# Two float32-split matmul layers on one core: the modulation's shift of the raw attention projections added on ScalarE, and the last slab's two output tiles made one behind the other

## The reference

```
def modulate(h, shift, scale):
    return h * (1 + scale[:, None, :]) + shift[:, None, :]
...
    mod = c_act @ w_mod[l] + b_mod[l]
    sh1, sc1, ga1, sh2, sc2, ga2, sh3, sc3, ga3 = jnp.split(mod, N_MOD, axis=-1)
    h = modulate(rms_norm(x, g_ffn1[l]), sh1, sc1)
    x = x + 0.5 * (1 + ga1[:, None, :]) * swiglu(h, w1_gate[l], w1_up[l], w1_down[l])
    h = modulate(rms_norm(x, g_mix[l]), sh2, sc2)
    x = x + (1 + ga2[:, None, :]) * hybrid_mixer(h, w_in[l], b_f[l], g_q[l], g_k[l], w_o[l])
    h = modulate(rms_norm(x, g_ffn2[l]), sh3, sc3)
    x = x + 0.5 * (1 + ga3[:, None, :]) * swiglu(h, w2_gate[l], w2_up[l], w2_down[l])
```

## Time and profile before

| what | value |
|---|---|
| median of 3 runs | 819.49 us (819.26 to 819.83) |
| profiled execution, its own time | 819.52 us |
| its span | 817.3 us |
| busy: TensorE matmul, VectorE, ScalarE | 802.3, 644.4, 487.0 us |
| qkv3 and o3, 495 to 620: TensorE, VectorE, ScalarE busy | 121.5, 93.4, 79.0 of 125 us |
| TensorE's granted clock | 1.00 in every stretch |

### The profile page before, as it was taken

The page is one execution under the profiler, slowest core; times in us unless marked ns, Lnnn a source line. Parts: engine busy times, 40 slices in busy tenths (PEclk is TensorE's granted clock), DMA queues, the critical chain, the costliest instruction groups (busy, mean ns, idle before and its releaser), DMA issues.

```text
span 817.3 us, 16917 instructions
## 1 busy us (share of the span) xinstructions
PE 802.3 (98%) x6862; PEld 780.7 (96%) x6862; DVE 644.4 (79%) x1333; ACT 487.0 (60%) x1015; POOL 21.2 (3%) x53
## 2 busy tenths in 40 slices
PE   7999999999999999999999999899999999999998
PEld 7999998999999999999999999889889999999998
DVE  5788887888899887999988786977667896775551
ACT  6754566767767565756554556665655775555440
POOL 1000000000000000000000000700000000000000
PEclk9999999999999999999999999999999999999999
DMA  8777673765565998489998887545334578665540
GB/s 290 260 234 226 200 267 128 235 199 188 189 225 166 324 308 286 144 295 336 361 333 292 288 263 222 167 134 175 120 118 156 156 249 274 207 199 194 194 155 27
DMA packets 150013, 179.44 MB, mean 220 GB/s; under 512 B 5680, under 2 KB 139568, under 8 KB 149936
## 3 DMA queue, kind: packets, MB, share of 16 engines
q1 hardware_dynamic: 147680, 177.22, 65.8%
q10 hardware_dynamic: 1232, 1.11, 0.4%
q0 software_dynamic: 1024, 0.03, 0.1%
HBM read 177.27 MB, written 1.05 MB: 218 GB/s over the span
## 4 chain that ended last, share of the span: by engine, by line
PE 77%; DVE 4%; ACT 2%; issue 1%; DVEq 0%; ACTq 0%
PE bank L1349 24%; PE bank L1352 24%; PE bank L1353 24%; DVE wlo L970 1%; PE bank L1451 1%; PE bank L1439 1%; PE bank L1468 0%; PE bank L1370 0%; PE bank L1402 0%; DVE yb L1010 0%; PE bank L1418 0%; DVE A L1021 0%; ACT B L748 0%; PE bank L1395 0%; ACT sq L768 0%
## 5 line engine op out<-in xcount | busy, mean ns | idle before, releaser
L970 DVE TENSOR_TENSOR wlo<-raw,whi 128x512 fp32r<-128x512 f32 x528 | 342.7, 683 | 69.4 <-ACT whi L727 68.7
L727 ACT ACTIVATE whi<-raw 128x512 fp32r<-128x512 f32 x528 | 307.3, 622 | 97.1 <-PE bank L1353 85.2
L1349 PE MATMUL bank<-A,whi 128*128 128x256 f32 x1264 | 357.3, 283 | 3.4 <-DVE wlo L970 2.6
L1352 PE MATMUL bank<-A,whi 128*128 128x256 f32 x1264 | 350.6, 277 | 0.1
L1353 PE MATMUL bank<-A,wlo 128*128 128x256 f32 x1264 | 350.2, 277 | 0.0
L1349 PEld LDWEIGHTS bank<-A,whi 128*128 128x128 f32 x1264 | 237.7, 188 | 6.5 <-DVE wlo L970 3.5
L1352 PEld LDWEIGHTS bank<-A,whi 128*128 128x128 f32 x1264 | 237.7, 188 | 1.2 <-issue 1.0
L1353 PEld LDWEIGHTS bank<-A,wlo 128*128 128x128 f32 x1264 | 237.8, 188 | 0.0
L1349 PE MATMUL bank<-Hhi,whi 128*128 128x256 f32 x528 | 146.2, 277 | 0.0
L1353 PE MATMUL bank<-Hhi,wlo 128*128 128x256 f32 x528 | 145.9, 276 | 0.0
L1352 PE MATMUL bank<-Hlo,whi 128*128 128x256 f32 x528 | 145.9, 276 | 0.0
(11 more groups left out here) (150 smaller groups left out, 811.0 us busy)
## 6 DMA issues: line engine op xcount, KB each, us to landing
mring<-in_w_mod SPq DMA_DIRECT2D x72, 512.0 KB, 6.4
raw<-in_ffn_w_up SPq DMA_DIRECT2D x22, 1024.0 KB, 5.1
raw<-in_w_gate SPq DMA_DIRECT2D x22, 1024.0 KB, 5.7
raw<-in_w_up SPq DMA_DIRECT2D x22, 1024.0 KB, 6.0
raw<-in_w_down SPq DMA_DIRECT2D x16, 1024.0 KB, 5.4
raw<-in_w_in SPq DMA_DIRECT2D x12, 1024.0 KB, 5.4
raw<-in_moba_w_qkv SPq DMA_DIRECT2D x11, 1024.0 KB, 5.5
raw<-in_ffn_w_down SPq DMA_DIRECT2D x8, 1024.0 KB, 6.2
```

The costliest lines, as they stand in the source:

```text
L727: act.activation(whi[:, i % SPL, k0:k1, 0:width], raw[:, i % RAW, k0:k1, 0:width], ACT.Copy).then_inc(s_whi, 1)
L970: dve.tensor_tensor(lo, raw[:, i % RAW, k0:k1, 0:width], hi.bitcast(F32), ALU.subtract).then_inc(s_wlo, 1)
L1349: pe.matmul(o, hi, xh, start=kg == 0 and not (j and halved(g)), stop=False)
L1352: pe.matmul(o, hi, xl, start=False, stop=False)
```

## The change

In a raw group of qkv, VectorE now multiplies by Rr and the scale in one instruction, and copies the two columns of the shift, scaled, from PSUM to a small tile shiftc. The bank is free behind that. ScalarE adds the column as a bias, in place on the QKV tiles, in a step of its own, `shift`, which the plan puts two turns behind the group's end, behind that turn's weight steps and ahead of `attend`: shift 69 behind hi 89 3, shift 70 behind hi 90 3, shift 71 behind hi 91 3 and so ahead of scores 16. TensorE's scores and V transpositions of raw groups now wait for these additions too.

In the last slab TensorE makes output tile 6 over all six k-tiles and then tile 7. VectorE adds tile 6 to x when it is ready, and tile 7 at the end.

```
 def evict(g):                                   # plan
             if tag == "qkv":
                 st.put("evict", g, 0)
+                if g in self.unnormed:
+                    shifts.append((g, turns[0]))
...
                     if i > 0:
                         fill(pieces(tag, c0, kt))
+                    while shifts and shifts[0][1] < turns[0]:
+                        st.put("shift", shifts.pop(0)[0])
                     attend()
...
+        shiftc = sb("shiftc", [P, 4, 2])
...
+        raw_g = {g: k for k, g in enumerate(g for g, x in enumerate(groups) if g in unnormed and x[1] == "qkv")}
...
+        def in_place(need, g):
+            emptied(need, g)
+            if g in raw_g:
+                need.wait_ge(s_biased, 2 * raw_g[g] + 2)
...
+            def add_shift(g):                   # ScalarE
+                base = qkv_base(groups[g][0], groups[g][2])
+                emptied(need, g)
+                for i in range(2):
+                    x = QKV[:, place(groups[g][0], base) + i, :]
+                    act.activation(x, x, ACT.Identity, bias=shiftc[:, raw_g[g], i:i + 1]).then_inc(s_biased, 1)
...
             def evict(g, part):                 # VectorE
-                if part == 0 and g not in by_silu:
+                if g == len(groups) - 1:
+                    need.wait_ge(s_ahead, 1)
+                elif part == 0 and g not in by_silu:
                     need.wait_ge(s_chunk, chunk_of_group(g))
...
                     for i in range(2):
-                        dve.tensor_tensor(QKV[:, place(ph, base) + i, :], at(g, i), Rr[:, 0, :], ALU.mult).then_inc(s_scaled, 1)
+                        dve.scalar_tensor_tensor(out=QKV[:, place(ph, base) + i, :], in0=at(g, i), scalar=scl,
+                                                 in1=Rr[:, 0, :], op0=ALU.mult, op1=ALU.mult).then_inc(s_scaled, 1)
                     for i in range(2):
-                        o = QKV[:, place(ph, base) + i, :]
-                        need.wait_ge(s_scaled, 2 * mul_g[g] - 1 + i)
-                        ins = dve.tensor_scalar(o, o, at(g, i, S, S + 1), scl, ALU.add, ALU.mult)
+                        ins = dve.tensor_scalar(shiftc[:, raw_g[g], i:i + 1], at(g, i, S, S + 1), scl, None, ALU.mult)
                     ins.then_inc(s_evicted, 1)
...
                         else:                   # down4's eviction
+                            if n == KD - 1:
+                                need.wait_ge(s_chunk, chunk_of_group(g))
...
+            def last_slab(i, kt):               # TensorE
+                ph, tag, c0, k0, nk = slabs[i][:5]
+                g = plan.group_of[i]
+                for j, k in [(0, kt)] + [(1, k) for k in range(nk if kt == nk - 1 else 0)]:
+                    final = k == nk - 1
+                    xh, xl, ncol = here(tag, ph, k0 + k, g)
+                    hi = whi[:, i % SPL, k, j * P:j * P + P]
+                    lo = wlo[:, i % SPL, k, j * P:j * P + P]
+                    o = at(g, j, 0, ncol)
+                    pe.matmul(o, hi, xh, start=False, stop=False)
+                    pe.matmul(o, hi, xl, start=False, stop=False)
+                    ins = pe.matmul(o, lo, xh, start=False, stop=final)
+                    if j == 0 and final:
+                        ins.then_inc(s_ahead, 1)
+                    elif final or (j == 0 and k % 2 == 1):
+                        ins.then_inc(s_chunk, 1)
...
             def scores(n):
-                emptied(need, max(qkv_group[ph, f], qkv_group[ph, 8 + f]))
+                for tile in sorted((f, 8 + f), key=lambda t: qkv_group[ph, t]):
+                    in_place(need, qkv_group[ph, tile])
...
             def v_turn(ph, tile):
-                emptied(need, qkv_group[ph, tile])
+                in_place(need, qkv_group[ph, tile])
```

More of the change, by code:

```diff
@@ L195, in lay @@
         offer(2)
-        pending, waiting, flight, scaling = [], [], [], []
+        pending, waiting, flight, scaling, shifts = [], [], [], [], []
         turns = [0]
@@ L503, in build_program @@
         s_xeven, s_xscaled = sem("s_xeven"), sem("s_xscaled")
+        s_ahead, s_biased = sem("s_ahead"), sem("s_biased")
         s_cond, s_cact, s_msum, s_mod = sem("s_cond"), sem("s_cact"), sem("s_msum"), sem("s_mod")
@@ L834, in evict @@
                     if ph == "qkv3" and (4 <= base < 8 or 12 <= base < 16):
-                        emptied(need, g)
+                        in_place(need, g)
                         if nth("qkn", base) > 1:
@@ L953, in _ @@
                        "ccol": condition, "evict": evict, "fpart": forget, "scores": first_passes, "turn": turned, "later": later,
-                       "values": values, "vturn": v_turned, "qkn": qk_norm}
+                       "values": values, "vturn": v_turned, "qkn": qk_norm, "shift": add_shift}
             for step in st.list:
@@ L1343, in multiply @@
                     pe.matmul(banks[NORM_BANK][:, 511:512], meanf[:, :], meanf[:, 0:1], start=True, stop=True)
+                if i == len(slabs) - 1:
+                    last_slab(i, kt)
+                    return
                 for j in range(1 if tag == "f" else 2):
```

## The result

| | before | after |
|---|---|---|
| median | 819.38 us (4 runs, 819.06 to 819.83) | 829.07 us (4 runs, 829.04 to 830.64) |
| profiled execution, own time | 819.52 us | 830.64 us |
| its span | 817.3 us | 828.3 us |

The ratio is 1.0119, with a 95% interval of 1.0106 to 1.0131: the changed kernel is 1.2% slower, 9.7 us, where I had forecast 819.9 us.

What follows compares the result with a forecast made beforehand. TensorE, busy 98% of the 817.3 us span, was taken as the bound. 819.49 + 0.83 (qkv3) - 0.39 (last slab) = 819.9 us, not distinguishable from no change; range 818.2 to 820.9.

Steps and rivals of the forecast that it cites:

- Behind it: qkv3 after the transposition: ScalarE 0.92 us later, product loses 0.60 us, norm product 0.83 in all; shiftc's move counted as none.
- The two signs of being wrong: qkv3: the forecast would be wrong if the transposition came before 525.6 or the product near 531 did not wait.
- VectorE's and ScalarE's prices: qkv3's raw groups: 0.80 us of VectorE per group, 0.40 less than today; 0.82 us of ScalarE per pair of additions.
- The sum up to the transposition: qkv3: TensorE's first wait shrinks, but waits for the shifts return the gain; transposition at 526.05, exactly where it is today.
- the forecast instants: qkv3 start times: scores 523.07, transposition 526.05, product 531.24, norm product 544.95.
- The last slab: Kernel's end: last addition and store 0.4 us earlier, -0.4 us; landing unchanged, up to 0.2 more possible; order most likely free.
- (1): Rival, qkv3: ScalarE not in the way, VectorE's lead reaches TensorE, both waits shrink; 817.1 us; chance 0.13.
- (2): Rival, qkv3: columns cost VectorE as much as today's additions, 0.27 us each; slower, 821.1 us; 0.09 for loss over 1.6 us.
- (3): Rival, qkv3: a pause absorbs the shift's delay, so qkv3 gives 0 and the tail 0.4; 819.1 us; chance 0.25.
- (4): Rival, qkv3: first wait's 0.8 us survive to the end, second wait keeps its length; 818.3 us; chance 0.10.

Runs made afterwards that it cites:

- e2: Kernel before with only an unused 32-byte tile where shiftc lies; 829.11 us against 820.49, ratio 1.0110.
- e1: Changed kernel with the pad ahead of H 32 bytes shorter, so H and O return to their old places; 820.57 us against 820.49, ratio 1.0004.
- g1: Changed kernel with tiles back in place and group 71's shift done by VectorE in the eviction, as before; 820.00 us against 820.13, ratio 0.9998.
- e3: Kernel before with only the last slab's new order, no shiftc; 818.73 us against 820.49, ratio 0.9984.
- g2: g1 with group 71's shift, and TensorE's wait for it, left out altogether; 819.81 us against 820.13, ratio 0.9995.
- f3: Kernel before with A alone moved 32 bytes on, to -32 from the weights, H and O unmoved; 843.52 us against 820.17, ratio 1.0285.
- f2: Kernel before with weights whi and wlo moved 64 bytes on, so A, H and O lie at -128; 844.82 us against 820.17, ratio 1.0301.
- f1: Kernel before with every tile moved by 64 bytes, weights and moving tiles alike; 820.18 us against 820.17, ratio 0.9994.
- f6: Kernel before with H and O moved back by 32 bytes, to -96; 827.50 us against 819.43, ratio 1.0087.
- f5: Kernel before with H and O moved on by 128 bytes, to +64; 826.83 us against 819.43, ratio 1.0089.
- f4: Kernel before with H and O moved back by 64 bytes, to -128; 829.13 us against 820.17, ratio 1.0110.
- e4: Kernel before with H and O moved on by 64 bytes, to 0 from the weights; 831.70 us against 820.49, ratio 1.0140.

## Why the prediction was wrong

**The step that failed** is the last sentence of "Behind it": "The new tile shiftc takes 32 bytes and moves the tiles declared behind it; no row shows an effect of a tile's place, and I count none." I saw the move and priced it at nothing, with no bound. H lies at a single distance in the trace of before, so no row there could give its price. But that is a reason to leave the sum open by the tile's share of the matmuls: H carries 1584 of the 6862, so each 1% on its interval is worth 1.8 us. It was 4.4%, 7.9 us, which is more than all other terms together. The runs put in its place: a move of H and O by 32 bytes relative to the weights costs 8.6 us by itself (e2), and moving them back takes it away (e1). A row of before could have warned me. Matmuls over B, whose k-tiles lie at eight places, are longer than those over A (120.3 ns from start to start for 113.4 in up2), by more than their two further columns on 256 (0.8%) would suggest. No run says whether the places or the columns do it. The means of the page are 284 and 277 ns:

```profile
L1352 PE MATMUL bank<-A,whi 128*128 128x256 f32 x1264 | 350.6, 277 | 0.1
...
L1352 PE MATMUL bank<-B,whi 128*128 128x258 f32 (+1 forms) x184 | 52.3, 284 | 0.0
```

The two signs of being wrong that the prediction names, a transposition before 525.6 and a product without a wait, both stayed away: they look at qkv3 alone, where the forecast held.

**VectorE's and ScalarE's prices** were right: 0.80 us a group from the nearest row, 0.80 to 0.82 a pair.

**The sum up to the transposition, and behind it**, was right step by step. The scores came to wait 0.59 us for shift 70 (forecast 0.5), the transposition 1.74 for shift 71 (forecast 1.7), the product 0.37 (forecast 0.6), and in e1 these three and the norm product start within 0.1 us of the forecast instants. Forecast +0.83; slabs 88 to 91 of after sum to +0.83 (-0.80, +0.84, +0.64, +0.15). The handovers, not the engines' totals, decided: VectorE leads by 0.8 us, and ScalarE, which had no pause, takes it back and 0.8 us more. That is the direction in which the rule of the Trainium skill pointed ("ScalarE: Activation LUTs", Rules for kernel authors: additions belong on VectorE), and g1 agrees: with shift 71 on VectorE, qkv3 is 1.1 us shorter than in e1, 0.9 of it in slabs 88 to 91.

**The last slab** had the right mechanism with a term too small: 0.57 us (e3: 0.58) for 0.39. I had taken the landing as unchanged and given up to 0.2 us more as a bound, and that bound is what came. The traces put it where the bound was given for: the last store takes 2.04 us from issue to landing before and 1.85 to 1.86 in after, e1 and e3. That the first store's nearness slows it is the likely reading; no run varies that distance alone. The new order of the 36 matmuls cost nothing, 113.3 ns before and in e3.

**The rivals.** (1), VectorE's lead reaches TensorE, fell: both waits moved to ScalarE. (2), the columns as dear as additions, fell: 0.21 us for two. (3), the delay absorbed in qkv3, and (4), the first wait's 0.8 us kept, fell with the slabs' sum in the profile of after. By time alone e1 (ratio 1.0004, 0.9992 to 1.0017) can't tell the forecast from (3) or (4); the slab lengths do. None of the rivals had the tile's move.

**What stays open**: how the chip makes an interval depend on this distance; what sets the level where one distance has two, as in up1 of g2 and perhaps with f3's H; and whether the pattern repeats every 256 bytes. For that only one pair speaks: in f2 A lies at 384 and H at 128 modulo 1024, and their intervals are 118.6 and 118.7 ns. The runs of e2 give 8.6 us in all, and the three down phases 7.9 of them; where the rest lies isn't settled, since o1 alone takes 32.9 to 33.8 us in the profiles of kernels in which neither its code nor any distance differs (before, e1, e3, f1, g1, g2).

## What to carry to other kernels

A change that adds or resizes an SBUF tile also moves all tiles declared behind it: list those that TensorE reads, and keep their distance from the weight tiles with a pad (e1). Declaring the new tile last would move none of them; no run here tried it. When TensorE is busy for longer with the same count of matmuls at the same granted clock, count matmul starts in equal stretches of each phase, and sort the phases by the tile that they read. Work handed to an engine without a pause returns as a wait one step later; here only the last slab's half of the change was worth having (0.9984).

## What the runs showed of the hardware

The interval of 128x128 by 128x256 matmuls by the distance from the weight tiles to the moving tile (bytes, modulo 256), all at a granted clock of 1.00 in these stretches. Each value is the mean of a phase in one profiled execution:

| distance | interval, ns | from |
|---|---|---|
| -64 | 113.3 | before, e1, e3, f1, g1, g2 (H) |
| -64 | 117.8 | a stretch of up1 in after, e2, g2 (A); f3 (H) |
| -96 | 117.3 | f6 |
| +64 | 117.8 | f5 |
| -32 | 118.3 | after, e2 (H); f3 (A) |
| -128 | 118.7 | f2 (H; A 118.6), f4 (H) |
| 0 | 120.0 | e4 |

I had not expected any effect: 32 bytes in an otherwise unchanged program are worth 1.1% of its time, and the weights' move by 64 bytes 3.0%. The second row shows that the distance isn't all of it. The interval at +64 equals that second level, so whether +64 has a faster one too isn't known. In the phases that use one bank for both tiles (qkv1, o1, qkv3, o3), intervals of about 113.4 and 117.8 ns both occur within one execution of the kernel before; what picks one of them isn't known.
